# A fused two-block transformer kernel: the gated state mixer's gates worked out during the stage ahead of it, and its sums of logarithms as two products of rounded parts

## The reference, cut to what matters

```python
q = jax.nn.silu(q)
log_f = jnp.logaddexp(jnp.log(lbf), jnp.log1p(-lbf) + jax.nn.log_sigmoid(f_raw))
k = -jnp.expm1(log_f)
# per chunk:
cum = jnp.cumsum(lfc, axis=2)
attn = jnp.einsum("bhlk,bhsk,bhlsk->bhls", qc, kc, decay)      # decay = exp(cum_l - cum_s), s <= l
o = attn @ vc + (qc * jnp.exp(cum)) @ state
state = jnp.exp(last) * state + (kc * jnp.exp(last - cum)).T @ vc
o = grouped_rms_norm(o, norm_w, 4) * jax.nn.silu(g)
```

## Time and profile before

| | |
|---|---|
| median of 3 runs | 3304.05 us (3297.43 to 3308.53) |
| the profiled execution's own time | 3305.42 us |
| its span, first to last instruction | 3303.6 us |
| mean granted TensorE clock | 0.921 of full |
| SSD stage | about 2662 to 2781 us of the span |
| HGRN stage | about 2772 to 2945 us of the span |

### The profile page before, as it was taken

One profiled execution on the slowest core, in us unless ns is written; L12 is line 12 of the kernel. 1 busy time (PEld: TensorE's weight loads), 2 busy tenths in 40 slices (PEclk: granted clock), 3 DMA queues, 4 the chain that ended last, 5 costly groups with the idle time before them and its releaser, 6 DMA issues. The chain is left out here.

```text
span 3303.6 us, 52657 instructions
## 1 busy us (share of the span) xinstructions
PE 2917.9 (88%) x21080; PEld 2509.0 (76%) x21080; DVE 1923.4 (58%) x2347; ACT 1279.1 (39%) x1815; POOL 759.7 (23%) x472
## 2 busy tenths in 40 slices
PE   8999996998577799499999968799999977887898
PEld 7999994777345687388888857699999955666687
DVE  4365644776365433789889856420057777687511
ACT  3000003554355322378878844221111147453411
POOL 3222212332172000222222201032232142222300
PEclk9999997999578899699999989899999989896999
DMA  4466322000410832699999954332557652213411
GB/s 173 158 214 212 113 81 102 32 32 10 91 44 36 315 115 77 241 386 403 404 400 397 396 222 162 137 122 101 164 174 233 213 218 96 99 56 88 146 67 48
DMA packets 195726, 559.76 MB, mean 169 GB/s; under 512 B 26768, under 2 KB 100624, under 8 KB 169376
## 3 DMA queue, kind: packets, MB, share of 16 engines
q1 hardware_dynamic: 149712, 460.23, 38.4%
q10 hardware_dynamic: 35632, 66.01, 5.5%
q0 software_dynamic: 10208, 31.13, 3.1%
HBM read 440.19 MB, written 124.32 MB: 171 GB/s over the span
## 5 line engine op out<-in xcount | busy, mean ns | idle before, releaser
L386 PE MATMUL pin_psum<-pin_sb_w,pin_sb_hT 128*128 128x354 f32 (+1 forms) x5376 | 976.9, 344 | 15.8 <-DVE pin_sb_hT L332 6.1
L386 PEld LDWEIGHTS pin_psum<-pin_sb_w,pin_sb_hT 128*128 128x128 f32 x5376 | 937.6, 189 | 52.6 <-DVE pin_sb_hT L332 6.8
L4302 DVE TENSOR_TENSOR moe_sb_wlo<-moe_sb_raw,moe_sb_whi 128x2048 fp32r<-128x2048 f32 x192 | 433.9, 2287 | 71.1 <-ACT moe_sb_whi L4114 71.1
L4114 ACT ACTIVATE moe_sb_whi<-moe_sb_raw 128x2048 fp32r<-128x2048 f32 x192 | 365.8, 1917 | 104.7 <-PE moe_psum L4377 75.9
L309 ACT ACTIVATE pin_sb_xt<-pin_psum,pin_sb_ss 128x353 f32<-128x353 f32 (+1 forms) x112 | 63.8, 589 | 563.9 <-PE pin_psum L386 493.5
L361 DVE TENSOR_SCALAR pin_sb_xt<-pin_psum,pin_sb_ss 128x353 f32<-128x353 f32 (+1 forms) x112 | 69.0, 625 | 330.6 <-PE pin_psum L386 330.4
L262 POOL CAST pin_sb_w<-pin_sb_raw 128x2832 fp32r<-128x2832 f32 (+1 forms) x26 | 74.5, 2866 | 630.2 <-PE pin_psum L386 584.9
L4377 PE MATMUL moe_psum<-moe_sb_whi,moe_sb_xhi 128*128 128x512 f32 x512 | 204.6, 400 | 8.2 <-DVE moe_sb_xlo L4306 8.2
L4377 PE MATMUL moe_psum<-moe_sb_whi,moe_sb_xlo 128*128 128x512 f32 x512 | 201.4, 393 | 0.0
L4377 PE MATMUL moe_psum<-moe_sb_wlo,moe_sb_xhi 128*128 128x512 f32 x512 | 201.0, 393 | 0.0
L264 POOL TENSOR_TENSOR pin_sb_w<-pin_sb_raw,pin_sb_w 128x2832 fp32r<-128x2832 f32 (+1 forms) x26 | 187.8, 7222 | 3.9 <-issue 0.6
(11 more groups left out here) (714 smaller groups left out, 5725.8 us busy)
## 6 DMA issues: line engine op xcount, KB each, us to landing
moe_sb_raw<-in_w_gate SPq DMA_DIRECT2D x64, 1024.0 KB
moe_sb_raw<-in_w_up SPq DMA_DIRECT2D x64, 1024.0 KB, 8.0
moe_sb_raw<-in_w_down SPq DMA_DIRECT2D x64, 1024.0 KB, 7.6
scratch_proj<-pin_sb_xt ACTq DMA_DIRECT2D x16, 1412.0 KB, 6.5
scratch_proj<-pin_sb_xt ACTq DMA_DIRECT2D x12, 1792.0 KB, 6.2
pin_sb_raw<-in_w_in SPq DMA_DIRECT2D x15, 1412.0 KB, 6.9
pin_sb_raw<-in_w_in SPq DMA_DIRECT2D x11, 1792.0 KB, 9.0
scratch_ybuf<-moe_sb_yb ACTq DMA_DIRECT2D x32, 512.0 KB, 8.4
```

The source lines that it names most:

```text
L386: mm = te.matmul(ps[:, t, 0:cols], hT[a_part][:, k, t * P:(t + 1) * P], wt[b][w_part][:, k, :], start=(k == 0 and n == 0), stop=(k == KD - ...
L4114: s.activation(whi[q][:, :, :], raw[q][:, :, :], ACT.Copy).then_inc(hi, 1)
L4302: tt(wlo[q][:, :, :], raw[q][:, :, :], whi[q][:, :, :].bitcast(F32), ALU.subtract).then_inc(lo, 1)
```

## The change

1. ACT opens all eight tiles' gates, one tile a unit, in SSD units 4 to 11 (`open_gate(t)`). `logs` for both batches follow at SSD unit 14. So all of `F` is loaded at the start; `K`, `LF` and `F` are whole tensors and no longer pairs, and other buffers change places in the arena.
2. The sums of logarithms (`sum_logs`, `decays`) use `LF_hi`, a copy of `LF` in the rounded type float32r, and `LF_lo = LF - LF_hi`, rounded too. Every plain float32 product becomes two float32r products that are summed in PSUM. The masks are rounded once (`round_masks`, exact for 0 and 1).
3. That adds `round_logs` on ACT (after the SSD loop, and in HGRN unit 1) and `rest_of_logs` on DVE (in SSD unit 15, and in HGRN unit 2). `gates(1)` on DVE moves from unit 2 to unit 1, and `queries(1)` on ACT from unit 1 to ahead of the stage.
4. Two DMA loads wait for more (`h_sums` ahead of the loads of c, `scored` ahead of that of `tab`).

```diff
@@ scalar @@
-            def open_gates(i):
-                s.wait_ge(f_in[i], 16)
-                s.activation(part(K, i), part(F, i), ACT.Abs)
+            def open_gate(t):
+                s.wait_ge(f_in[batch_of(t)], 16)
+                s.activation(K[:, t, :], F[:, t, :], ACT.Abs)
                 s.drain()
-                s.activation(part(K, i), part(K, i), ACT.Exp, scale=-1.0)
-                s.drain()
+                s.activation(K[:, t, :], K[:, t, :], ACT.Exp, scale=-1.0)
+
+            def round_masks():
+                s.wait_ge(h_masks_in, 16)
+                s.wait_ge(ind_in, 16)
+                s.activation(sum_masks[:, :], h_masks[:, P:5 * P], ACT.Copy)
+                s.activation(ind_r[:, :], ind[:, :], ACT.Copy).then_inc(masks_a, 1)
+
+            def round_logs(i):
+                s.wait_ge(karg_d, i + 1)
+                s.activation(part(LF_hi, i), part(LF, i), ACT.Copy).then_inc(lf_hi, 1)
...
+                if 4 <= u < 4 + NT:
+                    open_gate(u - 4)
                 if u == UNITS - 2:
-                    open_gates(0)
-                    logs(0)
+                    s.drain()
+                    for i in range(2):
+                        logs(i)
...
+                if u == 12:
+                    round_masks()
-            queries(0)
+            round_logs(0)
+            for i in range(2):
+                queries(i)
             close_keys(0)
             square(UNITS - 1)
+            s.wait_ge(diag_p, UNITS)
             exponents(0)
             decays(0)
...
                 if u == 0:
                     roots(TAIL_TILES)
-                    open_gates(1)
-                    logs(1)
                 if u == 1:
-                    queries(1)
+                    round_logs(1)
                 if u == 2:
                     close_keys(1)
@@ vector @@
+            def rest_of_logs(i):
+                ve.wait_ge(lf_hi, i + 1)
+                tt(part(LF_lo, i), part(LF, i), part(LF_hi, i).bitcast(F32), ALU.subtract).then_inc(lf_lo, 1)
...
                 if u == UNITS - 1:
                     gates(0)
+                    rest_of_logs(0)
                 join(u)
...
+                if u == 1:
+                    gates(1)
                 if u == 2:
-                    gates(1)
+                    rest_of_logs(1)
@@ tensor @@
             def decays(i):
                 for n, (t, h) in enumerate((t, h) for t in range(BATCH[i].start, BATCH[i].stop) for h in range(HH)):
-                    mm = te.matmul(ps[:, SCORE, 4 * n:4 * n + 4], tile_of(LF, t)[:, h * HD:(h + 1) * HD], ind[:, :], start=True, stop=True)
+                    for z in (LF_hi, LF_lo):
+                        mm = te.matmul(ps[:, SCORE, 4 * n:4 * n + 4], z[:, t, h * HD:(h + 1) * HD], ind_r[:, :],
+                                       start=(z is LF_hi), stop=(z is LF_lo))
...
-                te.wait_ge(lf_d, batch_of(t) + 1)
+                te.wait_ge(lf_lo, batch_of(t) + 1)
                 if u:
                     te.wait_ge(exps, u)
                 for bank, i, m in ((MID, 1, mid), (MID, 0, lev), (SUM, 0, h_cum), (SUM, 1, suf)):
-                    mm = te.matmul(half(bank, i), m, tile_of(LF, t)[:, h_cols(q)], start=True, stop=True)
+                    for z in (LF_hi, LF_lo):
+                        mm = te.matmul(half(bank, i), m, z[:, t, h_cols(q)], start=(z is LF_hi), stop=(z is LF_lo))
@@ sync @@
-            load(F[0][:, :, :], COL_F, BATCH[0], f_in[0])
+            for i in range(2):
+                load(F[:, BATCH[i], :], COL_F, BATCH[i], f_in[i])
...
-            load(F[1][:, :, :], COL_F, BATCH[1], f_in[1])
+            sp.dma_start(h_nw[:, :], g["hgrn_norm_w_2"].partition_broadcast(P)).then_inc(h_nw_in, 16)
...
+            sp.wait_ge(h_sums, GROUPS * HEAD)
             for k, name in enumerate(("s5_c_re_2", "s5_c_im_2")):
...
             sp.wait_ge(scaled, h_UNITS)
+            sp.wait_ge(scored, h_UNITS)
             sp.dma_start(tab[:, :, :, :].rearrange("p k j c -> p (k j c)"), tables.out["tab"]).then_inc(tab_in, 16)
```

More of the change, by code:

```diff
@@ L2706, in state_mixes @@
         h_masks = put("h_masks", [P, 7 * P], own)
-        h_ident, lev, mid, h_cum, suf, cross, diag = (h_masks[:, i * P:(i + 1) * P] for i in range(7))
+        h_ident, cross, diag = (h_masks[:, i * P:(i + 1) * P] for i in (0, 5, 6))
         ind = put("ind", [P, 4], own + 896)
         Q = put("Q", [P, NT, W], own + 928)
-        F = [put("F0", [P, HEAD, W], own + 5024), put("F1", [P, NT - HEAD, W], home["xdt"])]
-        LF = [put("LF0", [P, HEAD, W], own + 6048), put("LF1", [P, NT - HEAD, W], home["seg"])]
@@ L2712, in state_mixes @@
-        K = [put("K0", [P, HEAD, W], own + 7072), put("K1", [P, NT - HEAD, W], home["xdt"] + 3072)]
-        e1, e2c, e2, e2n = (two(n, [P, HW], own + 8096 + 512 * i) for i, n in enumerate(("e1_", "e2c", "e2_", "e2n")))
-        e34 = two("e34_", [P, 2, HW], own + 10144)
-        dec = put("dec", [P, NT, HH, 4], own + 11168)
-        h_ss = put("h_ss", [P, 4, NT * HH], own + 11296)
-        T5 = two("T5_", [P, 2, P], own + 11424)
-        at = two("at", [P, 2, P], own + 11936)
-        h_junk = two("h_junk", [P, 2, HD], own + 12448)
@@ L2720, in state_mixes @@
-        h_nw = put("h_nw", [P, W], own + 12960)
+        F, K = (put(n, [P, NT, W], own + 5024 + 4096 * i) for i, n in enumerate(("F", "K")))
+        dec = put("dec", [P, NT, HH, 4], own + 13216)
+        h_ss = put("h_ss", [P, 4, NT * HH], own + 13344)
+        e34 = two("e34_", [P, 2, HW], home["seg"])
+        T5 = two("T5_", [P, 2, P], home["seg"] + 1024)
+        at = two("at", [P, 2, P], home["seg"] + 1536)
+        h_junk = two("h_junk", [P, 2, HD], home["seg"] + 2048)
+        h_nw = put("h_nw", [P, W], home["seg"] + 2560)
@@ L2721, in state_mixes @@
+        sum_masks = put("sum_masks", [P, 4 * P], own + 13472, F32R)
+        lev, mid, h_cum, suf = (sum_masks[:, i * P:(i + 1) * P] for i in range(4))
+        ind_r = put("ind_r", [P, 4], own + 13984, F32R)
+        LF_hi = put("LF_hi", [P, NT, W], own + 5024, F32R)
+        LF_lo = put("LF_lo", [P, NT, W], home["xbc"] + 8192, F32R)
         V = put("V", [P, NT, W], home["xbc"])
         h_S = two("h_S", [P, RING, HW], home["xbc"] + 4096)
-        qk = two("qk", [P, 4, HW], home["xbc"] + 8192)
@@ L2724, in state_mixes @@
-        T12, T34 = (two(n, [P, 4, P], home["xbc"] + 10240 + 1024 * i) for i, n in enumerate(("T12_", "T34_")))
+        LF = put("LF", [P, NT, W], home["xbc"] + 8192)
+        qk = two("qk", [P, 4, HW], home["xdt"])
+        T12, T34 = (two(n, [P, 4, P], home["xdt"] + 2048 + 1024 * i) for i, n in enumerate(("T12_", "T34_")))
+        e1, e2c, e2, e2n = (two(n, [P, HW], home["xdt"] + 4096 + 512 * i) for i, n in enumerate(("e1_", "e2c", "e2_", "e2n")))
         G = put("G", [P, NT, W], home["sm"])
@@ L3407, in h_norm @@
                 ins.then_inc(h_normed, 1)
-            for q in range(GROUPS):
-                ve.memset(at[q][:, :, :], 0.0)
             ve.wait_ge(exps_a, 1)
```

9 lines of the change are left out of this document (5 added, 4 removed).

## The result

The changed kernel takes 3315.07 us (median of 9 runs) against 3306.39 us for the kernel before on the same chip; the ratio is 1.0034, 95% interval 1.0022 to 1.0045. It is slower by a third of a per cent, some 11 us. One of the nine runs was disturbed (3421.78) and is left out of the ratio. The profiled execution took 3320.03 us with a span of 3317.9, 14.3 us more than the span of before (3303.6).

The account below looks back on a forecast made before the run. PE, busy 88% of the span, was the first suspect, with ACT and DVE limiting some stretches. The terms, 0.3 + 3.2 - 2.95 - 3.7 - 1.2 = -4.35 us against the median 3304.05, gave 3299.7, say 3300 us; range 3291 to 3311.

Parts of the forecast that it names:

- the first rival: Regular part of the HGRN stage: longer PE waits make the clock fall, 2.84 us each, deciding from five falls; chance 0.17.
- Term 1: SSD stage: the added Abs and Exp mostly fit ACT's gaps, one delay of DVE is charged; +0.3 us.
- Term 2: Opening of the HGRN stage: second sums start later but run shorter, +2.75 us, plus 0.5 for half clock; +3.2 us.
- Terms 3 and 4: HGRN units 1 and 2: ACT's batch-1 gates leave unit 1, DVE has one shorter pass in unit 2; -2.95 and -3.7 us.
- Term 5: HGRN unit 3 and after: shorter sums win 0.5 us, later units 0.7, regular units 0; -1.2 us.
- Term 6: DMA loads: early F, later `tab` and SP's wait for the sums cost nothing; 0 us.
- Rounded products are cheaper: `decays(1)` in the HGRN stage: faster weight loads shrink its 48 records from 7.56 us, result 3296 to 3292; chance 0.16.
- The rounded sums gain nothing: HGRN sums: at 164 ns or worse per product, or if cold stretches move, up to 3 us lost, 3303; chance 0.15.
- The opening gives it all back: HGRN opening: four hand-overs between ACT and DVE cost 1 us more each, sum 0, result 3304; chance 0.07.

Follow-up runs that it names:

- e5_fill_in_wait: The changed kernel with eight more, unread products per unit in PE's wait ahead of the transposes; ratio 0.9999 to the kernel before, median 3298.72 us.
- e12_fill_behind_wait: The changed kernel with eight more, unread products per unit behind PE's wait, directly ahead of the transposes; ratio 1.0055 to the kernel before, 3322.84 us.
- e3_before_short: The kernel before, gates in place, with logarithms written rounded, low parts left out and eight rounded sum products per unit; ratio 1.0028, 3315.82 us.
- e9_rounded_gates_plain: The changed kernel with plain sums, DVE writing logarithms rounded, low parts left out and 24 rounded decay products; ratio 0.9970 to the kernel before, 3294.41 us.
- the kernel with one part: The changed kernel without low parts or their subtraction, each sum product issued four times, 16 per unit; ratio 0.9966 to the kernel before, 3290.82 us.

## Why the prediction was wrong

The forecast was 3300 us, range 3291 to 3311, with 0.08 for slower; it came out at 3315. What happened is the first rival, which got 0.17. Its mechanism stood in the text; its place only in part, since five of the eight losses lie outside the four norm units that it counted first, and its price of 2.84 us was the upper end (measured 1.5 to 3.0).

**Term 1 (+0.3) held by what it named.** From ACT's first instruction of the SSD stage to the end of the last `decay` it was 110.0 us and is 110.8. DVE's wait for `seg` in the SSD units was 1.57 us as before, and the one that was 2.78 is now (timeline of DVE)

```profile
2742.69 1.85 DVE L3320 TENSOR_TENSOR states_sb_seg<-states_sb_seg,states_sb_sm 128x1024 f32<-128x1024 f32 x1 [2.85 <-ACT states_sb_seg L3045]
```

**Term 2 (+3.2) measured +6.9**: +4.7 up to the first transposes, where 2.75 stood, and +2.2 in unit 0, where 0.5 stood for the next groups at half clock. The timeline of ACT:

```profile
2769.22 1.06 ACT L3045 ACTIVATE states_sb_seg<-states_sb_seg 128x1024 f32<-128x1024 f32 x1
...
2778.83 1.06 ACT L3072 ACTIVATE states_sb_LF_hi<-states_sb_LF 128x1024 fp32r<-128x1024 f32 x1 [1.74 <-DVE states_sb_K L3358]
...
2787.99 0.58 ACT L3096 ACTIVATE states_sb_e<-states_psum 128x512 f32<-128x512 f32 x1
```

From the end of the last `decay` to the first exponent are 17.7 us; the text worked out 16.2 (before: 11.5). The 1.5 us that it missed are ACT's wait: it took `LF` and `K` as done by the time of the rounding, but DVE was busy with the SSD stage's last unit and only came to the gates at 2776.25. DVE itself had waited there for PE (its timeline):

```profile
2774.86 0.69 DVE L3333 TENSOR_TENSOR states_sb_y<-states_sb_y,states_psum 128x512 f32<-128x512 f32 x1 [1.27 <-PE states_psum L3697]
```

PE's 16 products at that place (L3697) took 3.52 us, at half clock, against 1.89 before. That is chance in part: e5_fill_in_wait and e12_fill_behind_wait, whose code is the same up to there, had them at full clock, and their first exponent came 15.7 us after the last `decay`. The second sums took 2.04 us at half clock, as priced (1.9). Unit 0 ran at half clock, 8.35 us in place of 6.15: the stretch that brings the clock back was shorter, as the text said, and the 1.5 us that it kept as the upper end were too few.

**Terms 3 and 4 (-2.95 and -3.7) held.** The timeline of DVE:

```profile
2798.20 0.42 DVE L3383 TENSOR_TENSOR states_sb_qk<-states_sb_Q,states_sb_e 128x256 f32<-128x256 f32 x1
...
2799.87 3.35 DVE L3356 SCALAR_TENSOR_TENSOR states_sb_LF<-states_sb_F,states_sb_K 128x3072 f32<-128x3072 f32 x1
...
2814.22 0.42 DVE L3383 TENSOR_TENSOR states_sb_qk<-states_sb_Q,states_sb_e 128x256 f32<-128x256 f32 x1
2814.55 0.42 DVE L3384 TENSOR_TENSOR states_sb_qk<-states_sb_K,states_sb_e 128x256 f32<-128x256 f32 x1
...
2815.89 3.35 DVE L3362 TENSOR_TENSOR states_sb_LF_lo<-states_sb_LF,states_sb_LF_hi 128x3072 fp32r<-128x3072 f32 x1
```

`scale(1)` to `scale(2)` is 16.02 us (text: 15.9), and by the turns units 1 and 2 became 3.6 and 3.8 us shorter.

**Term 5 is the step that failed.** It said "In the regular units 0: `scale` covers it" and allowed -1.2 for all after unit 3. The first half is right in what it says of the path: at full clock, units 8 to 10 take 6.9, 7.0 and 8.6 us before and after, so shorter sums win nothing. But the cover is a wait, and a longer wait had a price of its own. Units 3, 4, 7, 11, 12 and 13 and the last unit's end lost 2.1 + 2.3 + 3.0 + 1.5 + 1.5 + 2.1 + 2.5 = 15.0 us, units 5 and 6 gave 0.5 back: +14.5 where -1.2 stood.

The loss has two forms. In the norm units 11 to 13 the wait ahead of the transposes grew and the clock fell there. (Unit 4 and the end of the last unit fell after waits of 1.53 and 1.56 us, no longer than the 1.57 at which the kernel before kept its clock; at the last one the kernel with doubled sums fell too and lost 1.5 of the 2.5 us.) In units 0, 3 and 7 it had fallen before, and it came back later. Ahead of unit 7, PE waits 2.43 us for a copy both in the changed kernel (up to 2873.01) and in the one with doubled sums (up to 2865.60), and both run at half clock then. The changed kernel's windows behind it:

```profile
2880.00:2884.00 4.00, 4.00 (x31) 2.78 (x30) 1.06 (x4) 1.04 (x6) 0.09 (x1) 0.50 0.00 1
2884.00:2887.00 3.00, 3.00 (x21) 2.87 (x22) 2.22 (x8) 0.71 (x2) 0.00 (x0) 0.68 0.00 0
```

and those of the one with doubled sums:

```profile
2868.00:2872.00 4.00, 4.00 (x24) 3.65 (x24) 1.75 (x6) 1.22 (x4) 0.27 (x1) 0.56 0.55 221
2872.00:2875.00 3.00, 3.00 (x38) 2.24 (x37) 1.79 (x6) 1.65 (x7) 2.37 (x3) 1.00 0.00 1
```

The one is at half clock for some 13 us, the other for some 6. Term 2 had priced this for the opening ("it leaves the next groups at half clock a little longer"); term 5 left it out for the later units. The runs show the cause of both forms: doubling the sums, or filling the wait, takes 12 to 15 us off again.

**Term 6 (0) is not decided.** Behind the stage the changed kernel took 2.66 us more. But this stretch lasts from 358.8 to 364.8 us in the profiled executions, and the 364.8 are of e3_before_short, which has neither of the two loads that wait for more.

**Where the weighing went astray.** The text put the decision at five falls of 2.84 us. (Its sum for four is wrong by 4: 3299.7 + 11.4 is 3311, not 3307.) There were eight places with a loss at half clock (units 0, 3, 4, 7, 11, 12, 13 and the last unit's end), at 1.5 to 3.0 us. It also had the wait right, 2.3 us in the norm units (measured 1.97 and 2.23), next to the row of the unit at 2856.86, where the clock fell after 1.71 us. The argument against was that 1.45 us leaves the clock alone in four norm units (in the trace the four waits are 1.19 and three times 1.45, and the last turn has 1.57, without a fall too). But no norm unit was going to keep 1.45: between rows up to 1.57 without a fall and one at 1.71 with a fall, 2.3 lies on the side of the falls. Going by the nearer row, this case would have been the likeliest in four or five norm units; three of them fell. The row at 1.71 is no limit, though: e9_rounded_gates_plain has a turn at 2837.05 after 1.72 us of wait, at full clock and in a unit of 6.92 us, and e3_before_short one after 2.23. The rule cited there (the Trainium skill, "TensorE: Matmul & The Clock Gate", Part 4: transposes do not count as busy in the way matmuls do) is not tested by these runs; what they show is that products ahead of the transposes keep the clock and the same products behind the wait do not in the norm units.

**The other rivals.** "Rounded products are cheaper" fell: records of 4 columns with rounded operands follow one another every 111 ns at full clock (24 take 2.84 us in the kernel with one part), the plain ones every 115. The faster weight load of the Trainium skill ("TensorE: Matmul & The Clock Gate", "Weight-path perf modes", for types other than FP32) does not show for this type: the estimate from that page for 48 records was 1.2 us, and the chain of the changed kernel, with more than half of them at half clock, has

```profile
2832.72 8.49 PE states_psum L3704 x48
```

"The rounded sums gain nothing" had the wrong reason: at 0.12 us a record they are as cheap as I took them (119 ns), and gain nothing because the path does not run through them. "The opening gives it all back" came nearer than its 0.07: term 2 was 3.7 us over the forecast, where it asked for 4, but by one wait and the half clock of unit 0, not by four hand-overs.

## What to carry over

An engine's wait that "covers" a saving is not free if the engine is TensorE. The saved work may have kept the clock up, or brought it back sooner after a fall. Read how long TensorE is quiet before the next product on the path, now and after the change, and look for the nearest row on either side at which the granted clock fell. If the new wait lies past one with a fall, charge the fall for most such places, not for all: after 2.23 us the clock fell in one turn of e3_before_short and held in the turn before. And a change of two halves is worth splitting: here one half wins 10 us and the other loses 21, 15 of them by the clock.

## What the runs showed of the hardware

A gapless stream of narrow products did not hold the clock. In the kernel with doubled sums the decays in unit 3 are 48 products of 4 columns without a gap, and the clock falls in the middle of them (timeline of PE):

```profile
2830.22 0.25 PE L3704 MATMUL states_psum<-states_sb_ind_r,states_sb_LF_hi 128*128 128x4 f32 x1
2830.33 0.25 PE L3704 MATMUL states_psum<-states_sb_ind_r,states_sb_LF_lo 128*128 128x4 f32 x1
2830.45 0.27 PE L3704 MATMUL states_psum<-states_sb_ind_r,states_sb_LF_hi 128*128 128x4 f32 x1
2830.58 0.35 PE L3704 MATMUL states_psum<-states_sb_ind_r,states_sb_LF_lo 128*128 128x4 f32 x1
2830.79 0.35 PE L3704 MATMUL states_psum<-states_sb_ind_r,states_sb_LF_hi 128*128 128x4 f32 x1
2831.00 0.35 PE L3704 MATMUL states_psum<-states_sb_ind_r,states_sb_LF_lo 128*128 128x4 f32 x1
```

They are 0.11 us apart up to 2830.45 and 0.21 us after 2830.58: PE was occupied all the time and the clock still went to half. And a rounded product of 256 columns takes 119 ns where a plain one takes 450 (two records, 1.80 us / 4), nearly a quarter; at 4 columns it is 111 against 230, only a half, since the plain product's two records are as long each as the rounded one's single.
